# Rotation tables of a state-space branch as products of two 16-entry tables, in a fused transformer kernel

## The reference

```python
dt = jnp.exp(log_dt.astype(f32))[:, None]
mag = jnp.exp(lr * dt)
ar, ai = mag * jnp.cos(li * dt), mag * jnp.sin(li * dt)
...
bu_r = jnp.einsum('blgh,gph->blgp', uf, bbr)
bu_i = jnp.einsum('blgh,gph->blgp', uf, bbi)
...
_, _, xr, xi = lax.associative_scan(combine, (a_r, a_i, bu_r, bu_i), axis=1)
y = (jnp.einsum('blgp,ghp->blgh', xr, c_re.astype(f32))
     - jnp.einsum('blgp,ghp->blgh', xi, c_im.astype(f32)))
```

## Time and profile before

| | |
|---|---|
| median of 3 runs | 1241.56 us (1241.49 to 1247.09) |
| the profiled execution | 1245.72 us, its span 1243.9 us |
| granted TensorE clock, mean | 0.959 |
| PE / DVE / ACT / POOL busy | 1144.2 / 772.0 / 619.9 / 173.1 us |

### The profile page before, as it was taken

The page is one execution under the profiler, slowest core; times in us unless marked ns, Lnnn a source line. Parts: engine busy times, 40 slices in busy tenths (PEclk is TensorE's granted clock), DMA queues, the critical chain, the costliest instruction groups (busy, mean ns, idle before and its releaser), DMA issues.

```text
span 1243.9 us, 21859 instructions
## 1 busy us (share of the span) xinstructions
PE 1144.2 (92%) x8526; PEld 1063.6 (86%) x8526; DVE 772.0 (62%) x1148; ACT 619.9 (50%) x1101; POOL 173.1 (14%) x260
## 2 busy tenths in 40 slices
PE   5987879898999999989988899999988799999997
PEld 4876657798999999989955699999986669999997
DVE  3699884465566566666455375666666657665663
ACT  4643334554455455464454364554554476454553
POOL 2399992010010000010000010000010001000000
PEclk8988788999999999999988899999999899999999
DMA  7424112335266766546430055666675405566650
GB/s 248 142 97 142 62 35 68 102 99 173 68 191 192 202 175 181 163 149 185 130 94 1 1 170 165 173 202 188 183 135 136 102 1 169 154 186 202 178 160 34
DMA packets 218142, 169.05 MB, mean 136 GB/s; under 512 B 20787, under 2 KB 208098, under 8 KB 217954
## 3 DMA queue, kind: packets, MB, share of 16 engines
q1 hardware_dynamic: 216962, 164.44, 45.5%
q0 software_dynamic: 496, 2.43, 0.5%
q10 hardware_dynamic: 624, 1.35, 0.4%
HBM read 167.15 MB, written 1.05 MB: 135 GB/s over the span
## 4 chain that ended last, share of the span: by engine, by line
PE 74%; DVE 15%; ACT 7%; issue 2%; SPq 1%; DMA 1%; POOL 0%; POOLq 0%; ACTq 0%; DVEq 0%
PE bank L1926 20%; PE bank L1928 19%; PE bank L1927 19%; PE bank L1989 11%; DVE wlo L1332 4%; DVE arena L1325 3%; ACT whi L787 2%; DVE arena L1478 1%; DVE arena L1516 1%; PE bank L1983 1%; PE bank L1985 1%; PE bank L1984 1%; ACT arena L1280 1%; SPq L662 1%; DVE hf L1343 1%
## 5 line engine op out<-in xcount | busy, mean ns | idle before, releaser
L1926 PE MATMUL bank<-mem_hi,whi 128*128 128x256 f32 x1408 | 407.5, 289 | 8.0 <-DVE mem_lo L1625 5.8
L1927 PE MATMUL bank<-mem_lo,whi 128*128 128x256 f32 x1408 | 401.0, 285 | 0.0
L1928 PE MATMUL bank<-mem_hi,wlo 128*128 128x256 f32 x1408 | 400.8, 285 | 0.0
L1926 PEld LDWEIGHTS bank<-mem_hi,whi 128*128 128x128 f32 x1408 | 273.0, 194 | 11.6 <-issue 8.7
L1926 PE MATMUL bank<-act_hi,whi 128*128 128x256 f32 (+1 forms) x920 | 265.3, 288 | 12.5 <-DVE act_lo L1351 4.4
L1927 PEld LDWEIGHTS bank<-mem_lo,whi 128*128 128x128 f32 x1408 | 272.9, 194 | 1.9 <-issue 1.7
L1928 PEld LDWEIGHTS bank<-mem_hi,wlo 128*128 128x128 f32 x1408 | 272.7, 194 | 0.0
L1927 PE MATMUL bank<-act_lo,whi 128*128 128x256 f32 (+1 forms) x920 | 261.4, 284 | 0.0
L1928 PE MATMUL bank<-act_hi,wlo 128*128 128x256 f32 (+1 forms) x920 | 261.3, 284 | 0.0
L1332 DVE TENSOR_TENSOR wlo<-raw,whi 128x1024 fp32r<-128x1024 f32 (+3 forms) x137 | 165.0, 1247 | 109.3 <-ACT whi L787 107.7
L1700 DVE TENSOR_TENSOR wlo<-raw,whi 128x1024 fp32r<-128x1024 f32 x177 | 208.8, 1220 | 3.9
(11 more groups left out here) (211 smaller groups left out, 1195.5 us busy)
## 6 DMA issues: line engine op xcount, KB each, us to landing
raw<-in_ffn_w_in_dram SPq DMA_DIRECT2D x132, 512.0 KB, 5.2
raw<-in_ffn_w_out_dram SPq DMA_DIRECT2D x33, 1024.0 KB, 5.0
raw<-in_w_in_ab_dram SPq DMA_DIRECT2D x11, 1024.0 KB, 5.3
raw<-in_w_in_dram SPq DMA_DIRECT2D x9, 1024.0 KB, 6.9
raw<-in_xa_wk_dram SPq DMA_DIRECT2D x4, 1024.0 KB, 5.7
raw<-in_xa_wv_dram SPq DMA_DIRECT2D x4, 1024.0 KB, 5.1
raw<-in_w_out_dram SPq DMA_DIRECT2D x4, 1024.0 KB, 5.1
raw<-in_xa_wq_dram SPq DMA_DIRECT2D x4, 1024.0 KB, 5.1
```

What stands on the lines that cost most here:

```text
L1926: pe.matmul(dst, w[0], a[0], start=start, stop=False, **kw)
L1927: pe.matmul(dst, w[0], a[1], start=False, stop=False, **kw)
L1928: return pe.matmul(dst, w[1], a[0], start=False, stop=stop, **kw)
```

## The change

The tables are no longer made by doubling. With t = 16 i + j, cos and sin of t times the angle follow from those of 16 i and of j times the angle. DVE makes the phases of both 16-entry tables (`phase`, from the angle and 16 times the angle, each reduced to (-pi, pi); the constant `steps` holds 0 to 15), ACT takes their sine and half-angle sine, DVE makes the cosine, and POOL multiplies the two tables out, six instructions of 128 x 1024 a half. The small tables and the phases lie in `bu`, so ACT's first `bu_out` waits for `s_rotr` = 2. `rot_tmp` grows to four chunks of `xkn`. The reduction becomes a function, `reduce`, and POOL no longer waits for `s_angle`.

```diff
@@ constants @@
+    cols.append(("steps", np.tile(np.arange(16.0), (P, 1))))
@@ gpsimd @@
-            wr, wi, w0, w1 = (ssm_col[:, k, 0:4] for k in range(17, 21))
             pool.wait_ge(s_coef, 3)
-            pool.wait_ge(s_angle, 4)
             for half, rot_ in enumerate((rot_early, rot_late)):
                 states = slice(4 * half, 4 * half + 4)
-                pool.tensor_copy(wr, ssm_col[:, 6, states])
-                pool.tensor_copy(wi, ssm_col[:, 4, states])
-                pool.memset(rot_[:, 0, :, 0:1], 1.0)
-                step(pool.memset(rot_[:, 1, :, 0:1], 0.0))
-                n = 1
-                while n < T:
...
-                    mul(c2, c, wrb)
-                    mul(s2, s, wrb)
-                    step(mul(tmp, s, wib))
-                    step(pool.tensor_tensor(c2, c2, tmp, ALU.subtract))
-                    step(mul(tmp, c, wib))
-                    n *= 2
-                    last = pool.tensor_tensor(s2, s2, tmp, ALU.add)
-                    if n < T:
-
-                        mul(w0, wr, wr)
-                        step(mul(w1, wi, wi))
-                        step(mul(wi, wr, wi))
-                        pool.tensor_scalar(wi, wi, 2.0, None, ALU.mult)
-                        step(pool.tensor_tensor(wr, w0, w1, ALU.subtract))
-                last.then_inc(s_rotr, 1)
+                ones_c, ones_s = (x[:, 0, states, :].unsqueeze(2).to_broadcast([P, 4, 16, 16]) for x in (turn_cos, turn_sin))
+                tens_c, tens_s = (x[:, 1, states, :].unsqueeze(3).to_broadcast([P, 4, 16, 16]) for x in (turn_cos, turn_sin))
+                c, s_ = (rot_[:, k, :, :].rearrange("p a (i j) -> p a i j", i=16) for k in range(2))
+                tmp = rot_tmp.rearrange("p a (i j) -> p a i j", i=16)
+                mul(c, tens_c, ones_c)
+                step(mul(tmp, tens_s, ones_s))
+                step(pool.tensor_tensor(c, c, tmp, ALU.subtract))
+                mul(s_, tens_s, ones_c)
+                step(mul(tmp, tens_c, ones_s))
+                pool.tensor_tensor(s_, s_, tmp, ALU.add).then_inc(s_rotr, 1)
                 pool.wait_ge(s_rotr, half + 1)
@@ scalar @@
             act.activation(half_sin, angle, ACT.Sin, scale=0.5).then_inc(s_angle, 1)
+            act.activation(turn_sin, phase, ACT.Sin).then_inc(s_angle, 1)
+            act.activation(turn_cos, phase, ACT.Sin, scale=0.5).then_inc(s_angle, 1)
             act.preload_act_table_set(LN_EXP_TABLES)
...
+                if s == 0:
+                    act.wait_ge(s_rotr, 2)
@@ vector @@
+            def reduce(x, tmp):
+
+                step(dve.tensor_scalar(tmp, x, 1 / (2 * math.pi), ROUND, ALU.mult, ALU.add))
+                step(dve.tensor_scalar(tmp, tmp, -ROUND, None, ALU.add))
+                for part in PARTS:
+                    step(dve.scalar_tensor_tensor(x, tmp, -part, x, ALU.mult, ALU.add))
+
...
-            dve.tensor_scalar(angle, t0, BOUND, -BOUND, ALU.min, ALU.max).then_inc(s_coef, 1)
+            reduce(t0, turns)
+            dve.tensor_scalar(angle, t0, BOUND, -BOUND, ALU.min, ALU.max)
+            step(dve.tensor_scalar(t1, t0, 16.0, None, ALU.mult))
+            reduce(t1, turns)
+            steps16 = const("steps").unsqueeze(1).to_broadcast([P, 8, 16])
+            for w, x in enumerate((t0, t1)):
+                step(mul(phase[:, w], x.unsqueeze(2).to_broadcast([P, 8, 16]), steps16))
+            reduce(phase, phase_tmp)
+            dve.tensor_scalar(phase, phase, BOUND, -BOUND, ALU.min, ALU.max).then_inc(s_coef, 1)
...
-            dve.wait_ge(s_angle, 4)
+            dve.wait_ge(s_angle, 6)
+            step(mul(turn_cos, turn_cos, turn_cos))
+            dve.tensor_scalar(turn_cos, turn_cos, -2.0, 1.0, ALU.mult, ALU.add)
             step(mul(t0, half_sin, half_sin))
             dve.tensor_scalar(cos_, t0, -2.0, 1.0, ALU.mult, ALU.add).then_inc(s_coef, 1)
```

More of the change, by code:

```diff
@@ L370, in build @@
         conv_o = prod[0]
-        rot_tmp = xkn[:, 6:8, :].rearrange("p c t -> p (c t)")[:, 0:4 * P]
+        rot_tmp = xkn[:, 4:8, :]
+        turn = bu.rearrange("p a b t -> p (a b t)")[:, 0:512].rearrange("p (f w s n) -> p f w s n", f=2, w=2, s=8)
+        turn_cos, turn_sin = turn[:, 0], turn[:, 1]
+        phase, phase_tmp = (bu.rearrange("p a b t -> p (a b t)")[:, 512 + 256 * k:768 + 256 * k].rearrange("p (w s n) -> p w s n", w=2, s=8)
+                            for k in range(2))
         tap_product = xkn[:, 7, :]
@@ L378, in build @@
         after_probs = used[0]
-        late = room(3202 - early_consts, at=after_probs)
+        late = room(3218 - early_consts, at=after_probs)
         after_late = used[0]
@@ L701, in mul @@
                 return pool.tensor_tensor(dst, a, b, ALU.mult)
-            wr, wi, w0, w1 = (ssm_col[:, k, 0:4] for k in range(17, 21))
             pool.wait_ge(s_coef, 3)
-            pool.wait_ge(s_angle, 4)
             for half, rot_ in enumerate((rot_early, rot_late)):
                 states = slice(4 * half, 4 * half + 4)
-                pool.tensor_copy(wr, ssm_col[:, 6, states])
-                pool.tensor_copy(wi, ssm_col[:, 4, states])
-                pool.memset(rot_[:, 0, :, 0:1], 1.0)
-                step(pool.memset(rot_[:, 1, :, 0:1], 0.0))
-                n = 1
-                while n < T:
-                    c, s = rot_[:, 0, :, 0:n], rot_[:, 1, :, 0:n]
-                    c2, s2 = rot_[:, 0, :, n:2 * n], rot_[:, 1, :, n:2 * n]
-                    wrb = wr.unsqueeze(2).to_broadcast([P, 4, n])
-                    wib = wi.unsqueeze(2).to_broadcast([P, 4, n])
-                    tmp = rot_tmp[:, 0:4 * n].rearrange("p (a t) -> p a t", a=4)
-                    mul(c2, c, wrb)
-                    mul(s2, s, wrb)
-                    step(mul(tmp, s, wib))
-                    step(pool.tensor_tensor(c2, c2, tmp, ALU.subtract))
-                    step(mul(tmp, c, wib))
-                    n *= 2
-                    last = pool.tensor_tensor(s2, s2, tmp, ALU.add)
-                    if n < T:
-                        mul(w0, wr, wr)
-                        step(mul(w1, wi, wi))
-                        step(mul(wi, wr, wi))
-                        pool.tensor_scalar(wi, wi, 2.0, None, ALU.mult)
-                        step(pool.tensor_tensor(wr, w0, w1, ALU.subtract))
-                last.then_inc(s_rotr, 1)
@@ L1401, in _ @@
             step(mul(t0, li, dt_))
+            def reduce(x, tmp):
[3 more added lines that the diff above has]
+                    step(dve.scalar_tensor_tensor(x, tmp, -part, x, ALU.mult, ALU.add))
             ROUND = 1.5 * 2.0 ** 23
             PARTS = (6.28125, 0.0019340515136718750, 2 * math.pi - 6.28125 - 0.0019340515136718750)
-            step(dve.tensor_scalar(t1, t0, 1 / (2 * math.pi), ROUND, ALU.mult, ALU.add))
-            step(dve.tensor_scalar(turns, t1, -ROUND, None, ALU.add))
-            for part in PARTS:
-                step(dve.scalar_tensor_tensor(t0, turns, -part, t0, ALU.mult, ALU.add))
             BOUND = 3.1415925
-            dve.tensor_scalar(angle, t0, BOUND, -BOUND, ALU.min, ALU.max).then_inc(s_coef, 1)
+            reduce(t0, turns)
[7 more added lines that the diff above has]
+            dve.tensor_scalar(phase, phase, BOUND, -BOUND, ALU.min, ALU.max).then_inc(s_coef, 1)
             for i in range(2):
```

## The result

| | before | changed | ratio, 95% interval |
|---|---|---|---|
| median (range) | 1243.63 us (1241.49 to 1247.09, 4 runs) | 1259.95 us (1255.94 to 1262.76, 4 runs) | 1.0128 [1.0091, 1.0165] |
| profiled execution | 1245.72 us, span 1243.9 | 1262.76 us, span 1260.8 | +17.0 us |

The account below looks back on a forecast made before the run. PE's matmuls dominate the chain, with DVE the bound from 57 to 111 us. Terms +26.2 + 1.0 + 2.8 + 2.2 + 4.4 - 11.5 = +25.1 us on the median 1241.56 give 1267; range 1256 to 1277.

Parts of the forecast that it names:

- main term: DVE's work up to the convolution's product alternates with POOL's twelve long instructions, so the product ends 26.2 us late.
- product for the convolution late: DVE's product for the convolution ends at 90.4 instead of 64.19 us, behind POOL's twelve instructions: +26.2 us.
- hand-off to the second norm: PE stands still from about 70 us and restarts colder, up to the second norm: +1.0 us (0 to 4).
- taps: DVE's 20 taps lie beside POOL's taps at 0.92 us each, 19.3 us with the norm instead of 16.5: +2.8 (0 to 5).
- eight splits: Eight weight splits on DVE before 153 us take 1.44 instead of 1.16 us each beside POOL's taps: +2.2 us.
- quarter 0: DVE's first state quarter, now beside POOL's taps, takes 14.6 instead of 10.2 us: +4.4 us.
- given back: With POOL through before quarter 1, quarters 1 to 3 take 10.2 us and PE's waiting for DVE goes: -11.5 us.
- The start: DVE's and ACT's new small-table work makes the coefficient event, and POOL's start, 4.7 us late (bounds 3 to 6).
- Rival 1: Short DVE instructions pass POOL's long ones, only nine wide ones wait about 3 us each: 1259 us, chance 0.12.
- turn-taking in the quarters: DVE and POOL alternate instructions with fixed parts overlapping, so a quarter beside POOL's taps takes 15.0 us at most.
- rule of whole instructions: The shared port is held for whole instructions, so DVE's taps cost 8 us more and the time is 1275.

Follow-up runs that it names:

- e4: Changed kernel with POOL's twelve rotation instructions replaced by a constant fill, so tables are wrong: 1237.77 us, ratio 0.9948 to the kernel before.
- e3: Changed kernel with each of POOL's twelve 1024-wide instructions split into four of 256: 1250.81 us, ratio 1.0036 to the kernel before.
- e1: Changed kernel with POOL's twelve rotation instructions starting only after DVE has the convolution's gated input: 1258.25 us, ratio 1.0099 to the kernel before.
- e10: Kernel before with four taps moved from POOL to DVE and 16 small PE matmuls ahead of quarters 1 to 3's output products: 1240.42 us, ratio 0.9961.
- e5: Kernel before with 16 small PE matmuls ahead of the output products of quarters 1 to 3: 1246.36 us, ratio 1.0023.
- e9: Kernel before with four taps moved from POOL to DVE (12 instead of 8 on DVE): 1244.33 us, ratio 0.9998.
- e8: Changed kernel with POOL's 23 taps starting only when quarter 0 is done: 1259.42 us, ratio 1.0127 to the kernel before.

## Why the prediction was right or wrong

The direction and the mechanism of the main term held. The measured 1259.95 us lies in the range of 1256 to 1277, but not in 1262 to 1272, to which the forecast gave 0.68; it was 9 us too high by the times and 8 by the profiles. From A to C, where the sum's terms lie, the profiles differ by only 12.1 us; the other 4.8, ahead of A and behind C, brought the total nearer to the forecast and are no merit of it. By the steps of its own sum, with what the profile of the changed kernel shows:

| step | forecast | measured, and from what |
|---|---|---|
| (not in the sum) ahead of A | 0 | +2.3 |
| product for the convolution late | +26.2 | +22.7 (63.50 to 88.55, less the 2.3) |
| hand-off to the second norm | +1.0 | +2.1 (6.99 us to 9.13) |
| from there to the taps | 0 | -0.3 |
| taps | +2.8 | -2.7 (16.56 us to 13.91) |
| eight splits | +2.2 | +1.9 (+0.9 with the norm to B, +1.0 before quarter 1) |
| quarter 0 | +4.4 | +4.7 (10.2 us to 14.9) |
| eleven taps behind quarter 0 | 0 | +1.8 (5.74 us to 7.51) |
| given back | -11.5 | -18.3 (quarter 1 to C: 70.92 us to 52.67) |
| behind C | 0 | +2.4 |

Unrounded, the right column adds up to 16.8.

**The main term** was right in kind: the short coefficient instructions wait for POOL's long ones. e4 shows that POOL's twelve are the cause, e3 that their length sets the wait, and e1 that the place does not matter. It was 3.5 us too large, in three parts. The start cost 3.7 us at the event that starts POOL (49.76 to 55.83, less the 2.3), not 4.7: a one-input instruction of 256 takes 0.29 us, not the estimated 0.40, and the fused ones 0.45, not 0.53. The twelve took 28.35 us where 28.8 were forecast. And from their end to the product's it took 5.05 us, not 7.1. The forecast let each of DVE's first twelve instructions wait; but of the thirteen two-input ones of 8 elements five slip in at 0.17 us (68.03, 74.43, and one in each of the pairs at 61.72, 70.53 and 74.63), so all of them were through and the second pair of splits was under way when POOL ended at 84.18. (The rows from which the twelve were priced go on to 1.94 and 2.41 us at 1024, which is 26.4 us with the gaps and not 27.2, and 23.3 and not 22 for the lower bound; measured were 1.92 to 1.95 and 2.35 to 2.41 where no split stood beside them.)

**Rival 1** gave 1259, the number that was measured, by a mechanism that did not happen: nine of the fourteen 8-wide instructions with two inputs or of the kind TENSOR_SCALAR did wait, 1.8 to 2.4 us each. A total that fits proves no step.

**The taps** failed in sign, 5.5 us off. The term let one DVE tap pass for each POOL instruction, 0.92 us apiece. Groups by line of the stretch with DVE's taps, before (76.7 to 93.2 us) and changed (103.6 to 117.6): busy us, mean ns of one, idle before:

```profile
L1478 DVE SCALAR_TENSOR_TENSOR arena<-arena,tap 128x256 f32<-128x256 f32 x19 | 14.4, 756 | 0.6
```

```profile
L1482 DVE SCALAR_TENSOR_TENSOR arena<-arena,tap 128x256 f32<-128x256 f32 x19 | 12.0, 632 | 0.6
```

Beside POOL's taps one takes 632 ns: in a POOL pair of 2.0 us (104.74 to 106.74) three DVE taps end, not two. One of the pair is a product with one input, and one DVE tap more fits beside it; that this is why is inferred. Beside the old 256- and 512-wide rotations, where the kernel before had these taps, the mean is 756. POOL's side of the term was too small: its 23 taps took 53.9 us (102.72 to 156.58), not 48, since splits hold them up (the one-input product at 119.47 took 2.83 us beside them, 0.93 alone). They still ended before quarter 1.

**What was given back** was mis-sized by 6.8 us, the largest error of the sum: the taps come next, and then the main term. I took PE's waiting, 11.5 us, as its ceiling. PE's wait has a second cost: its next 20 matmuls are slower, 6.4 to 6.7 us instead of 3.83, so a wait of 3.5 to 4.2 us costs some 6.5. Three of these, 19.5 us at the most, bear out the measured 18.3, once POOL's taps are out of the way. Two profiles split the 18.3 another way: with a busy PE and POOL's taps ended early (e10) quarter 1 to C is 65.22 us, 5.7 less than before, while DVE's quarters are still long; the other 12.6 come with the quarters at 10.1 us each instead of 14.3 to 15.0. So PE's 11.5 us was no ceiling: DVE's own saving of some 13, which the forecast named and set aside, comes near the 12.6, and PE's slower matmuls and POOL's last tap come on top. And I wrote that the 3.55 us wait of the earlier trace rows "held nobody that I can find": e5 shows that it stood ready to hold DVE as soon as PE was quicker. A wait that is short now is the next bound when the one above it goes. Neither half alone won anything in the kernel before (e5, e9); in the changed kernel both went together.

**The turn-taking in the quarters**, chosen against the rule of whole instructions (1275), held: quarter 0 took 14.9 us where 14.6 was measured before beside the taps. e8 shows the same from the other side: 10.1 us without POOL. Beside the 1024-wide instructions, though, an 8-wide one that waits does wait for nearly the whole of POOL's.

**Hand-off:** PE stood still from 72 to 89 us as forecast (70 to 91), and its restart cost 2.1 us, twice the estimate.

## What to carry to other kernels

Fewer and longer instructions on POOL are cheaper on POOL and dearer for DVE: here a DVE instruction with two SBUF inputs that came while POOL had a 1024-wide one in hand waited for nearly the whole of it, so the price (22 us) was near the number of POOL's long instructions by their length (28 us), and narrow DVE instructions paid it as wide ones did. Before moving work to POOL, or merging POOL's work, count what DVE runs beside it; if those are narrow ones, keep POOL's instructions short or let DVE do the work, which took 1.2 us here against 1.9 to 2.4 for 1024 elements. And price a wait that goes by what follows it as well: the clock behind it, and the next wait that stands ready.

## What the runs showed of the hardware that was not expected

- An 8-wide TENSOR_SCALAR with one input also waited for POOL: 2.02 us (68.47) beside 1024-wide instructions, 0.55 beside 256-wide (e3), 0.17 beside none (e1), while the 8-wide RECIPROCAL took 0.20 in all three. The Trainium skill, page "SBUF — State Buffer", section "Who interferes with whom", names tensor_scalar among the operations that can take the shared pair of ports; the rows agree.
- A POOL fill of 2 x 2048 elements (3.67 us) left the two splits beside it at 2.36 us (e4).
- PE's group of 20 matmuls took 3.83 to 3.86 us after idle times up to 2.33 us, 5.52 after 3.51 and 5.88 after 5.29 in e9, 5.37 after 3.17 in e8, and 6.4 to 6.7 after 3.5 to 4.2 in the kernel before, in windows of a quarter each with a granted clock of 0.78 to 0.79 of full speed, between the two levels of 1.2 and 2.4 GHz; the changed kernel had 0.91 in its quarter 1.
